# Expert weights of the first mixture in rows of 4096 bytes

## The reference

```
logits = (x2 @ w_router) + b_router
top_vals, top_idx = lax.top_k(logits, TOP_K)          # 2 of 8 experts
gates = jax.nn.softmax(top_vals, axis=-1)
...
def expert_block(args):
    xb, e = args                                      # the tokens of expert e
    h = xb @ w_in[e]                                  # 1024 -> 2 * 2816
    return (jax.nn.silu(h[:, :D_FF]) * h[:, D_FF:]) @ w_out[e]
```

## Time and profile before

| | |
|---|---|
| time, median of 3 runs | 1906.64 us (1902.38 to 1908.56) |
| time of the profiled execution | 1904.77 us |
| its span, first to last instruction | 1903.0 us |
| granted TensorE clock over the span | 0.976 of full speed |
| TensorE busy | 1721.0 us, 90% |
| DMA traffic of the whole execution | 498.53 MB, 66424 packets |
| first mixture, from the first expert's matmuls to the last's | about 537 to 1220 us |

### The profile page before, as it was taken

The page is one execution under the profiler, slowest core; times in us unless marked ns, Lnnn a source line. Parts: engine busy times, 40 slices in busy tenths (PEclk is TensorE's granted clock), DMA queues, the critical chain, the costliest instruction groups (busy, mean ns, idle before and its releaser), DMA issues.

```text
span 1903.0 us, 53269 instructions
## 1 busy us (share of the span) xinstructions
PE 1721.0 (90%) x24496; PEld 1356.0 (71%) x24496; DVE 588.7 (31%) x1402; ACT 242.4 (13%) x625; POOL 160.0 (8%) x307
## 2 busy tenths in 40 slices
PE   8999999999999898988979798799989999989775
PEld 6758886467489898888979787687657778643331
DVE  1641000133332221212212122346764344233223
ACT  2321000032111000000000000022133112110000
POOL 0000000010003800000000000064520000000000
PEclk9999999999999999999999999999989999999898
DMA  7225343242479999999999999822211029589996
GB/s 308 109 89 199 138 172 133 90 178 89 168 298 417 399 417 363 421 402 408 415 416 410 389 416 377 340 89 78 70 53 41 30 79 384 208 326 429 429 429 274
DMA packets 66424, 498.53 MB, mean 262 GB/s; under 512 B 7480, under 2 KB 16208, under 8 KB 17488
## 3 DMA queue, kind: packets, MB, share of 16 engines
q1 hardware_dynamic: 56128, 490.12, 64.1%
q10 hardware_dynamic: 10128, 5.97, 1.1%
HBM read 495.00 MB, written 1.05 MB: 261 GB/s over the span
## 4 chain that ended last, share of the span: by engine, by line
PE 82%; DMA 7%; issue 5%; DVE 4%; ACT 1%; ACTq 1%; DVEq 0%; SPq 0%
PE pb L1205 20%; PE pb L825 11%; PE pb L1223 10%; PE pb L834 7%; PE pb L830 5%; PE pb L898 4%; PE pb L1083 3%; DMA ringbuf<-in_e2out 2%; PE pb L1453 2%; PE pb L1430 2%; PE pb L1719 2%; DMA arena<-in_e2in 2%; DMA ringbuf<-in_e2in 2%; PE pb L1441 2%; PE pb L1383 1%
## 5 line engine op out<-in xcount | busy, mean ns | idle before, releaser
L1205 PE MATMUL pb<-arena,ringbuf 128*64 128x72 f32 (+6 forms) x11264 | 388.6, 229 | 41.4 <-issue 41.1
L1205 PEld LDWEIGHTS pb<-arena,ringbuf 128*64 128x64 f32 x11264 | 375.8, 139 | 52.0 <-issue 51.5
L1781 DVE TENSOR_TENSOR arena<-arena,pb 128x256 f32<-128x256 f32 (+15 forms) x290 | 111.9, 409 | 738.2 <-ACT arena L2796 352.0
L1223 PE MATMUL pb<-arena,ringbuf 128*64 128x72 f32 (+6 forms) x5632 | 207.2, 230 | 30.0 <-issue 28.7
L1223 PEld LDWEIGHTS pb<-arena,ringbuf 128*64 128x64 f32 x5632 | 196.0, 140 | 33.1 <-issue 33.1
L825 PE MATMUL pb<-XT,ringbuf 128*128 128x256 f32 (+2 forms) x1104 | 201.6, 345 | 0.8 <-ACT XT L2604 0.8
L825 PEld LDWEIGHTS pb<-XT,ringbuf 128*128 128x128 f32 (+1 forms) x1104 | 180.0, 191 | 22.1 <-issue 2.1
L834 PE MATMUL pb<-arena 64*64 64x64 f32 (+9 forms) x664 | 105.6, 323 | 5.4 <-DVE Y L1781 2.9
L2604 ACT ACTIVATE arena<-pb 128x256 f32<-128x256 f32 (+8 forms) x156 | 65.2, 439 | 347.3 <-PE pb L1132 62.9
L2796 ACT ACTIVATE arena<-pb 128x144 f32<-128x144 f32 (+6 forms) x88 | 25.6, 291 | 607.1 <-PE pb L1205 607.1
L834 PEld LDWEIGHTS pb<-arena 64*64 64x64 f32 (+8 forms) x664 | 53.4, 153 | 54.3 <-issue 37.6
(11 more groups left out here) (413 smaller groups left out, 1850.1 us busy)
## 6 DMA issues: line engine op xcount, KB each, us to landing
ringbuf<-in_ein SPq DMA_DIRECT2D x176, 1024.0 KB, 9.0
ringbuf<-in_eout SPq DMA_DIRECT2D x88, 1024.0 KB, 9.2
arena<-in_e2in SPq DMA_DIRECT2D x13, 2048.0 KB, 25.7
ringbuf<-in_e2in SPq DMA_DIRECT2D x12, 2048.0 KB, 34.8
ringbuf<-in_fin SPq DMA_DIRECT2D x11, 2048.0 KB, 7.6
ringbuf<-in_e2out SPq DMA_DIRECT2D x8, 2048.0 KB, 30.7
ringbuf<-in_wo SPq DMA_DIRECT2D x6, 2048.0 KB, 7.7
arena<-in_e2out SPq DMA_DIRECT2D x6, 2048.0 KB, 33.2
```

The costliest lines, as they stand in the source:

```text
L1205: ins = pe.matmul(UP[f % 3][h_, t * n:(t + 1) * n], w3[:, k, (t % 2) * 128 + h_.start:(t % 2) * 128 + h_.stop], XG[e][:, k, :], start=k == ...
L1223: ins = pe.matmul(PB[d // 4][h_, (d % 4) * n:(d % 4 + 1) * n], w3[:, k, o:o + 64], HID[e][s % 3][:, k, :], start=k == 0, stop=k == 1)
L1781: return v.tensor_tensor(o, a, b, op)
```

## The change

The arrays `ein` and `eout` are stored with each tile as two blocks: the first halves of all 128 rows, then the second halves, so the tile in HBM is 2 x 128 rows of 4096 bytes, and the two halves of one partition lie 524288 bytes apart. The transfers keep their number, size, order, waits, semaphores and place in SBUF; the source and the destination are now described as 128 x 2 x 1024 floats where they were 128 x 2048. On every engine the instructions stand in the same order as before.

```
 def plan_o1(e):
-    return ([(dr["ein"][e, i].rearrange("x p n -> p x n"), SLOT) for i in range(11)],
-            [(dr["eout"][e].rearrange("i p (k n) -> p i k n", k=2)[:, :, :, 128 * d:128 * d + 128], DFF) for d in range(8)])
+    return ([(dr["ein"][e, i].rearrange("x a p n -> p (x a) n"), SLOT) for i in range(11)],
+            [(dr["eout"][e].rearrange("i k p n -> p i k n")[:, :, :, 128 * d:128 * d + 128], DFF) for d in range(8)])
...
-    sp.dma_start(IN1[s % 3][x], dr["ein"][who, f, x].rearrange("o p n -> (o p) n")).then_inc(in_sem[s % 3][x], 16)
+    sp.dma_start(IN1[s % 3][x].rearrange("p (a n) -> p a n", a=2), dr["ein"][who, f, x].rearrange("o a p n -> p (o a) n")).then_inc(in_sem[s % 3][x], 16)
...
-    sp.dma_start(OUT1[s % 3], dr["eout"][who, s % 11].rearrange("o p n -> (o p) n")).then_inc(out_sem[s % 3], 16)
+    sp.dma_start(OUT1[s % 3].rearrange("p (k n) -> p k n", k=2), dr["eout"][who, s % 11].rearrange("o k p n -> p (o k) n")).then_inc(out_sem[s % 3], 16)
...
-A["eout"] = np.stack([rowsk(w, 2) for w in I["w_exp_out"][0]])
+A["ein"] = np.ascontiguousarray(A["ein"].reshape(NE1, 11, 2, 128, 2, 1024).transpose(0, 1, 2, 4, 3, 5))
+A["eout"] = np.ascontiguousarray(I["w_exp_out"][0]).reshape(NE1, 11, 2, 128, 1024)
```

## The result

| | before | after |
|---|---|---|
| median | 1906.64 us (15 runs, 1902.38 to 1913.61) | 1914.65 us (15 runs, 1909.03 to 1920.34) |
| ratio | | 1.0035, interval 1.0023 to 1.0048 |
| profiled execution | 1904.77 us, span 1903.0 | 1912.62 us, span 1910.8 |

The change costs 6.7 us by the ratio (4.4 to 9.2 by its interval), 8.0 by the medians. That is slower by little, but the interval doesn't reach "no change". The forecast was 1907, with 1902 to 1911 as its own range and 1889 to 1919 as the range over all cases.

The account below looks back on a forecast made before the run. The first mixture was taken as bound by TensorE plus its instruction fetches, DMA engines close behind. 0.5 us for weights and 2 for fetches, the rest 0, made +2.5 on 1904.77: 1907, range 1889 to 1919.

Parts of the forecast that it names:

- What a tile costs: First mixture's weight transfers with a full queue: a tile goes from 2.491 to 2.557 us, 421 to 410 GB/s.
- Term 1: First mixture: idle DMA time and buffered weights hide slower tiles, except 0 to 2.4 us of waiting; 0.5 us taken.
- the named place: End of the 64-token expert's loop, where an `eout` tile lands with only 1.4 us to spare.
- the five experts: First-mixture window of 165 tiles, 421.66 us before: claimed 421 to 424 us, engines going from 404 to 410 GB/s.
- Term 2: TensorE's instruction fetches in the first mixture: weights ahead drain 2.7% slower, 0.04 us x 48 fetches, +2 us.
- Term 3: SyncE's 264 weight-transfer issues: even a doubled issue time hides beside 555.9 us of waiting, 0 us.
- term 4: Last mixture, attention and all other stages keep their transfers: 0 us.
- The faster rival: First mixture: shorter packets let instruction blocks through sooner, gain 14 to 21 us, time 1889; chance 0.21.
- The slower rival: First mixture: rate falls to 391 GB/s, TensorE waits for weights at loop ends, 12 us, time 1917; chance 0.21.
- The merged case: Weight transfers: rows merge again and all stays, 1905; chance 0.58 together with the main forecast.
- Gaps of 2.0 to 2.6 us: Sign of being right: TensorE's gaps behind each 128 matmuls of new code in the first mixture last this long.
- wrong if the gaps change by over 0.3 us each: Sign against the forecast: TensorE's instruction-fetch gaps in the first mixture change by more than this.

Follow-up runs that it names:

- near: Changed kernel's 4096-byte rows, but a row's two halves 4160 bytes apart in HBM in place of 524288: 1914.05 us, ratio 1.0034 to the kernel before.
- half: Kernel before, moving only the first half of each 8192-byte weight row from the fourth step on: 1831.02 us, ratio 0.9602.
- a3840: Changed kernel with rows of 3840 bytes in place of 4096 from the fourth step on: 1894.57 us, ratio 0.9943 to the kernel before.
- b7936: Kernel before with rows of 7936 bytes in place of 8192 from the fourth step on: 1896.93 us, ratio 0.9959.
- r2048: Expert weights in rows of 2048 bytes, four blocks of 128 rows in each tile, against the kernel before: 1941.88 us, ratio 1.0183.
- trim: Changed kernel with rows of 3984 bytes in place of 4096 from the fourth step on: 1913.47 us, ratio 1.0031 to the kernel before.

## Why the prediction was right, and where it was short

1. *What a tile costs* (2.491 to 2.557 us, 421 to 410 GB/s): right, 409 and 407 measured in the changed kernel and 404 to 410 in `near`. A transfer at the very start of the program had shown the new form's price before it was made, though only over 1.4 us. One reading was off: the slices of the first mixture stand at 340 to 421 GB/s in the earlier trace rows, not at 400 to 422.
2. *Term 1, weights against TensorE*: the wait came at the named place with 0.4 us in one profile of three, where 0 to 0.8 were expected; 0.5 was booked. But its picture of the five experts, 421 to 424 us with the engines going from 404 to 410 GB/s, was wrong: 428.1, 428.9 and 429.6 us in the three profiles, at 399 GB/s in the first. TensorE didn't ask for more, since it was itself delayed by term 2 and by its busy time.
3. *Term 2, instruction fetch*: right in mechanism, short in size. +2 us was booked, as 48 fetches of 0.04 us more each; +6.1 was measured. Part of it is a count: 48 blocks are those of the 500 us of the earlier trace rows, while q8 fetched 69 in the whole stage, before and after. That alone makes 2.8 us. The rest is not accounted for. The table counts 49 to 51 waits before the change and 51 to 55 behind it (50 and 53 on average), and a wait is 1.38 to 1.47 us long on average before and 1.39 to 1.50 behind it; both ranges meet or overlap, so whether more fetches fail to hide or each waits longer is not shown. The longer way of a tile (10.6 us in place of 9.0) would do either. No trace shows when a block was asked for. The evidence that a fetch is hidden when the engines are idle was thin as well: the 4 GB/s of the earlier trace rows cover the first 3.3 us of the 9.07 us of the earlier trace rows, and over all 9.07 us the engines moved 238 GB/s. It was `half` that showed it. The 3.3 us of busy time had no term.
4. *Term 3, SyncE, and term 4, the other stages*: 0 us, right. Waits of 527 us are left to SyncE, and the rest of the program takes what it took.
5. *The faster rival* is refuted by `a3840` and `b7936`. *The slower rival* gave 1917 by waiting for weights; there were 0.4 us of it. `r2048` shows it at 380 to 387 GB/s. *The merged case* is refuted by the packet count.
6. *"Gaps of 2.0 to 2.6 us"* held for the gaps shown (2.10, 2.26, 2.09), but this was a weak sign, and so was "wrong if the gaps change by over 0.3 us each": a look at single gaps would have called the cost nothing.

On the execution's basis the forecast said +2.5 us, and as 1907 against the median of 1906.64 it said next to nothing; the ratio says +6.7. The measured 1914.65 lies in the range that was to hold 8 in 10, but that range is wide because it takes in both rivals. It misses the forecast's own 1902 to 1911 and falls into the slower rival's 1912 to 1925, whose mechanism did not happen. In that sense the range held by luck. "Within 0.3%" (0.58) was the wrong side by a little: the measured +0.35% belongs to "slower" (0.22). Nothing tried here beats the kernel before with all its weights moved.

## What to carry to other kernels

When the DMA queue is full, "no one waits for data" doesn't make its occupancy free: straight-line code on TensorE fetches its instructions through the same engines, and here each per cent of occupancy cost about 2.8 us of 1907. Price it with one run that moves a few per cent less in the same number of packets, and see in its profile that the tile did get quicker, before arguing about packet sizes. And take the length of the whole stage, over several profiles: single gaps looked unchanged here, and the split into waits and busy time differed between executions of the same kernel.

## What the runs showed of the hardware

- The rate in full stretches by row length: 380 to 387 GB/s at 2048 bytes, 403 to 411 at 4096, 419 to 423 at 8192, 424 and 425 with `ein` at 16384.
- Rows of 3984 bytes run at 395 to 398 GB/s, less than rows of 4096, so that 2.7% fewer bytes took no less time; rows of 3840 bytes run at 408 to 410.
- The distance between the halves of a row makes no difference here: ratio 1.0034 at 4160 bytes, 1.0035 at 524288.
- TensorE's waits for instructions in this stage: 87.0 us with rows of 2048 bytes, 72.0 before, 30.1 at three quarters of the traffic, 13.1 at half. Its granted clock in the stage was 0.98 before and 1.00 at half the traffic; among kernels with tiles of the same length it was 0.99 in `near` (busy 612.6 us), 0.98 in the changed kernel (618.7) and 0.97 in `trim` (623.2).
